# Softmax division moved behind the attention products, and weight splits moved to GpSimd, in a hybrid encoder layer

## The reference, cut to what matters

```python
def _attention(q, k, v):                       # per sequence of 512 tokens, 8 query heads, 2 key/value heads, width 64
    s = jnp.einsum('bqkgd,bskd->bkgqs', qblk, k) * scale
    p = jax.nn.softmax(s, axis=-1)             # exp(s - max) / sum(exp(s - max)) over the 512 keys
    return jnp.einsum('bkgqs,bskd->bqkgd', p, v)
...
attn_out = _attention(q, k, v)
lru_out = h_lru * gelu(gate)                   # gated recurrence, 512 channels
mixed = concatenate([attn_out, lru_out])       # 1024 channels
x = x + einsum('bse,ed->bsd', mixed, w_out)    # output projection
... # then RMSNorm, a router that lets each of 16 experts choose 64 tokens, and three 1024x1024 products per expert
```

## Time and profile before

| | |
|---|---|
| time, median of 3 runs (lowest to highest) | 1011.89 us (1011.8 to 1012.08) |
| time of the profiled execution | 1012.73 us |
| its span from the first to the last instruction | 1010.7 us |
| PE busy | 981.9 us, 97% of the span |
| DVE, ACT, POOL busy | 830.2, 732.6, 173.2 us |
| granted PE clock over the span | 0.992 |

### The profile page before, as it was taken

The page is one execution under the profiler, slowest core; times in us unless marked ns, Lnnn a source line. Parts: engine busy times, 40 slices in busy tenths (PEclk is TensorE's granted clock), DMA queues, the critical chain, the costliest instruction groups (busy, mean ns, idle before and its releaser), DMA issues.

```text
span 1010.7 us, 15239 instructions
## 1 busy us (share of the span) xinstructions
PE 981.9 (97%) x5076; PEld 826.8 (82%) x5076; DVE 830.2 (82%) x1063; ACT 732.6 (72%) x982; POOL 173.2 (17%) x195
## 2 busy tenths in 40 slices
PE   8999999999999999969999999999999999999997
PEld 8997998877878788857888888888888888888885
DVE  6659898989885543667989998999999899989995
ACT  7447897487994334447878887888888788878873
POOL 1000000043793321250100110110011001101001
PEclk9999999999999999979999999999999999999999
DMA  7110111001102635379999999999999999999972
GB/s 269 49 43 21 37 38 43 1 1 64 63 2 66 213 121 177 118 267 398 409 391 392 390 412 392 392 393 409 392 392 405 397 392 391 410 392 392 390 273 62
DMA packets 75315, 248.98 MB, mean 246 GB/s; under 512 B 9421, under 2 KB 16649, under 8 KB 75273
## 3 DMA queue, kind: packets, MB, share of 16 engines
q1 hardware_dynamic: 70472, 231.12, 59.0%
q0 software_dynamic: 4784, 17.30, 6.5%
q10 hardware_dynamic: 16, 0.00, 0.0%
HBM read 231.63 MB, written 16.78 MB: 246 GB/s over the span
## 4 chain that ended last, share of the span: by engine, by line
PE 87%; DVE 5%; ACT 3%; DMA 2%; issue 2%; POOL 1%; POOLq 0%; ACTq 0%; DVEq 0%
PE bank L1097 25%; PE bank L1099 25%; PE bank L1098 25%; PE bank L1103 6%; DMA raw_gate<-in_exp_w_gate_dram 2%; PE bank L1263 1%; PE bank L1262 1%; PE bank L1295 1%; POOL prob L667 1%; DVE e_lo L1905 1%; PE bank L1147 1%; PE bank L1402 1%; POOL wo_lo L659 0%; DVE row_stat L1713 0%; ACT e_hi L1025 0%
## 5 line engine op out<-in xcount | busy, mean ns | idle before, releaser
L1097 PE MATMUL bank<-e_hi,xsT_hi 128*128 128x512 f32 x508 | 199.7, 393 | 1.3 <-DVE e_lo L1905 1.3
L1099 PE MATMUL bank<-e_hi,xsT_lo 128*128 128x512 f32 x508 | 197.8, 389 | 0.0
L1098 PE MATMUL bank<-e_lo,xsT_hi 128*128 128x512 f32 x508 | 197.8, 389 | 0.0
L1025 ACT ACTIVATE e_hi<-raw_gate 128x1024 fp32r<-128x1024 f32 x128 | 134.8, 1061 | 35.0 <-PE bank L1099 29.3
L1905 DVE TENSOR_TENSOR e_lo<-raw_gate,e_hi 128x1024 fp32r<-128x1024 f32 x126 | 149.5, 1221 | 6.1 <-ACT e_hi L1025 2.3
L1905 DVE TENSOR_TENSOR e_lo<-raw_down,e_hi 128x1024 fp32r<-128x1024 f32 x128 | 149.5, 1220 | 4.4 <-ACT e_hi L1025 1.4
L1905 DVE TENSOR_TENSOR e_lo<-raw_up,e_hi 128x1024 fp32r<-128x1024 f32 x128 | 148.4, 1220 | 4.5 <-ACT e_hi L1025 3.2
L1025 ACT ACTIVATE e_hi<-raw_down 128x1024 fp32r<-128x1024 f32 x128 | 128.4, 1060 | 11.8 <-PE bank L1099 11.8
L1025 ACT ACTIVATE e_hi<-raw_up 128x1024 fp32r<-128x1024 f32 x128 | 126.8, 1057 | 2.7 <-PE bank L1099 1.2
L1097 PEld LDWEIGHTS bank<-e_hi,xsT_hi 128*128 128x128 f32 x508 | 95.4, 188 | 22.1 <-DVE e_lo L1905 3.0
L1099 PEld LDWEIGHTS bank<-e_hi,xsT_lo 128*128 128x128 f32 x508 | 95.4, 188 | 19.9
(11 more groups left out here) (305 smaller groups left out, 2022.2 us busy)
## 6 DMA issues: line engine op xcount, KB each, us to landing
raw_gate<-in_exp_w_gate_dram SPq DMA_DIRECT2D x64, 1024.0 KB, 18.2
raw_up<-in_exp_w_up_dram SPq DMA_DIRECT2D x64, 1024.0 KB, 18.8
raw_down<-in_exp_w_down_dram SPq DMA_DIRECT2D x64, 1024.0 KB, 18.5
w_raw<-in_w_in_dram SPq DMA_DIRECT2D x6, 1024.0 KB, 5.4
wo_raw<-in_w_out_dram SPq DMA_DIRECT2D x8, 512.0 KB, 4.3
y_dram<-x SPq DMA_DIRECT2D x8, 512.0 KB, 5.2
h_rows<-h SPq DMA_DIRECT2D x8, 512.0 KB, 2.7
x_nat<-in_x_prompt_dram SPq DMA_DIRECT2D x4, 512.0 KB, 6.0
```

Source lines behind the costliest of these rows:

```text
L1025: act.activation(e_hi[:, (8 * m + j) % SPLIT, :], raw[:, j // 2, j % 2, :], ACT.Copy).then_inc(row_hi, inc)
L1097: pe.matmul(out, l_hi, r_hi, start=first, stop=False)
L1098: pe.matmul(out, l_hi, r_lo, start=False, stop=False)
L1099: return pe.matmul(out, l_lo, r_hi, start=False, stop=last)
```

## The change

The probabilities stay unnormalised: POOL no longer touches `prob`, and the transposes wait for the exponentials (`exp_done`). The division moves behind the products, once per pair. DVE takes the reciprocals of 8 units in one instruction; POOL spreads them over the head width (`spread_recip`); PE turns them, four transposes per pair (`spread_shares`, at the end of slot 8p + 15 for pair p); ACT copies them to `shares` (slot 8p + 16, in place of `mixA_hi`); and DVE multiplies the pair's bank by them into `high_half` (slot 8p + 17). POOL then makes `mixA_hi` and `mixA_lo` from `high_half`. `V_LAG` becomes 9. The high parts of the first 12 halves of `wo` and of the 8 pieces of `lru_out` move from ACT to POOL. Some semaphores of single engines are merged, which adds and removes no work.

```diff
-    T_LAG, V_LAG = 6, 8
+    T_LAG, V_LAG = 6, 9
+    SHARES_AT = {8 * pair + 6 + V_LAG: pair for pair in range(HEADS // 2)}
+    def shares_bank(pair):
+        return 7 if pair < PAIRS_ONE_BANK else out_bank(pair - 1)
+    def ended_pair(u):
+        v = u - V_LAG - 1
+        return v // (2 * BPS) if 0 <= v < UNITS and v % (2 * BPS) == 2 * BPS - 1 else None
...
 # POOL (link: wait for its own last instruction)
+        def spread_recip(pair):
+            pool.wait_ge(recip_done, pair + 1)
+            if pair:
+                pool.wait_ge(high_done, pair)
+            pool.tensor_copy(spread, shares_of.unsqueeze(3).to_broadcast([P, BPS, 2, HD])).then_inc(spread_done, 1)
+        def finish_pair(pair):
+            pool.wait_ge(high_done, pair + 1)
+            link(pool.tensor_copy(mixA_hi[mix_of(pair)], high_half[:, :]))
+            pool.tensor_tensor(mixA_lo[mix_of(pair)], high_half[:, :], mixA_hi[mix_of(pair)].bitcast(F32), ALU.subtract).then_inc(mixA_lo_done, 1)
...
-                pool.wait_ge(wo_hi_done, n + 1)
+                pool.wait_ge(wo_loaded[k], 16)
+                link(pool.tensor_copy(wo_hi[k][:, cols], wo_raw[k][:, cols]))
                 pool.tensor_tensor(wo_lo[k][:, cols], wo_raw[k][:, cols], wo_hi[k][:, cols].bitcast(F32), ALU.subtract).then_inc(wo_lo_pool, 1)
...
-                pool.wait_ge(mixL_hi_done, n - 2 * WO_EARLY + 1)
+                link(pool.tensor_copy(mixL_hi[:, i, cols], lru_out[:, i, cols]))
...
-                pool.wait_ge(recip_done, u + 1)
-                pool.tensor_scalar(prob[:, u % PROB_SLOTS, :], prob[:, u % PROB_SLOTS, :], row_stat[:, 2, u:u + 1], 1.0,
-                                   ALU.mult, ALU.mult).then_inc(prob_done, 1)
+            elif kind == "slot" and ended_pair(n - 1) is not None:
+                finish_pair(ended_pair(n - 1))
+            elif kind == "slot" and n + 4 in SHARES_AT:
+                spread_recip(SHARES_AT[n + 4])
...
 # ACT
-                    act.activation(mixA_hi[...], bank[:, out_bank(pair), :], ACT.Copy).then_inc(mixA_hi_done, 1)
+                    act.wait_ge(shares_turned, pair + 1)
+                    act.activation(shares[:, :], bank[:, shares_bank(pair), :], ACT.Copy).then_inc(shares_copied, 1)
...
 # PE
+                shared = sum(slot < slot_of_turn(n) + 1 for slot in SHARES_AT)    # in turn_heads
+                if shared:
+                    pe.wait_ge(shares_copied, shared)
...
-                pe.wait_ge(mixA_lo_done, pair if pair < PAIRS_ONE_BANK else pair - 1)
+                pe.wait_ge(high_done, pair if pair < PAIRS_ONE_BANK else pair - 1)
+                if pair >= PAIRS_ONE_BANK:
+                    pe.wait_ge(shares_copied, pair)
...
+        def spread_shares(pair):
+            pe.wait_ge(spread_done, pair + 1)
+            if shares_bank(pair) == 7:
+                before = [n for n in range(EARLY, USES * NB) if slot_of_turn(n) < 8 * pair + 6 + V_LAG]
+                pe.wait_ge(*turn_out(before[-1]))
+                pe.wait_ge(*turn_out(before[-2]))
+            else:
+                pe.wait_ge(high_done, pair)
+            transposes(shares_bank(pair), [spread[:, qb, :, :].rearrange("p h d -> p (h d)") for qb in range(BPS)], shares_turned)
...
-                    pe.wait_ge(prob_done, BPS * (head + 1))
+                    pe.wait_ge(exp_done, BPS * (head + 1))
...
 # DVE
-                    dve.tensor_tensor(mixA_lo[where], bank[:, out_bank(pair), :], mixA_hi[where].bitcast(F32), ALU.subtract).then_inc(mixA_lo_done, 1)
-                if 0 <= u - 1 < UNITS:
-                    dve.reciprocal(row_stat[:, 2, u - 1:u], row_stat[:, 1, u - 1:u]).then_inc(recip_done, 1)
+                    dve.wait_ge(pv_done, 2 * BPS * (pair + 1))
+                    dve.wait_ge(shares_copied, pair + 1)
+                    dve.tensor_tensor(high_half[:, :], bank[:, out_bank(pair), :], shares[:, :], ALU.mult).then_inc(high_done, 1)
+                if 0 < u - 1 <= UNITS and (u - 1) % (2 * BPS) == 0:
+                    dve.reciprocal(row_stat[:, 2, units], row_stat[:, 1, units]).then_inc(recip_done, 1)
```

More of the change, by code:

```diff
@@ L163, in layer_program @@
     assert VW * BPS * 4 == 5 * K
+    high_half = at("high_half", R1 + 95 * K, [P, S], F32)
+    shares = at("shares", R6 + 36 * K + 768, [P, S], F32)
+    spread = shares[:, :].rearrange("p (q h d) -> p q h d", q=BPS, h=2)
+    assert 3 * SEQS * HQ * BPS * 4 <= 768 and R6 + 38 * K + 768 <= nc.sbuf_usable_end - base
     QUIET = R1 + 48 * K
@@ L472, in out_bank, with mix_of @@
         return 6 if pair < PAIRS_ONE_BANK or pair % 2 == 0 else 7
+    def shares_bank(pair):
[3 more added lines that the diff above has]
+        return v // (2 * BPS) if 0 <= v < UNITS and v % (2 * BPS) == 2 * BPS - 1 else None
+    def mix_of(pair):
+        return slice(None), pair % (HQ // 2), slice(pair // (HQ // 2) * S, (pair // (HQ // 2) + 1) * S)
     def late_pair(v):
@@ L654, in _, with link @@
                 pool.memset(v[:, :, :].bitcast(F32).rearrange("p b (g d) -> p b g d", d=HD)[:, :, 0::2, :], 0.0).then_inc(v_zeroed, 1)
+        own = [0]
+        def link(ins):
+            own[0] += 1
+            ins.then_inc(pool_step, 1)
+            pool.wait_ge(pool_step, own[0])
+        def spread_recip(pair):
+            pool.wait_ge(recip_done, pair + 1)
+            if pair:
+                pool.wait_ge(high_done, pair)
+            shares_of = row_stat[:, 2, 2 * BPS * pair:2 * BPS * (pair + 1)].rearrange("p (h q) -> p q h", h=2)
+            pool.tensor_copy(spread, shares_of.unsqueeze(3).to_broadcast([P, BPS, 2, HD])).then_inc(spread_done, 1)
[3 more added lines that the diff above has]
+            pool.tensor_tensor(mixA_lo[mix_of(pair)], high_half[:, :], mixA_hi[mix_of(pair)].bitcast(F32), ALU.subtract).then_inc(mixA_lo_done, 1)
         for kind, n in attn:
@@ L923, in _ @@
                 act.activation(small[:, 122:123], eps, ACT.Exp)
-            elif kind == "split_hi":
-                if n < 2 * WO_EARLY:
-                    split_wo_hi(n // 2, n % 2)
-                else:
-                    i, cols = (n - 2 * WO_EARLY) // 2, slice(n % 2 * S, (n % 2 + 1) * S)
-                    act.wait_ge(scores_done, BPS * HQ)
-                    act.wait_ge(gated, SEQS * CT)
-                    act.activation(mixL_hi[:, i, cols], lru_out[:, i, cols], ACT.Copy).then_inc(mixL_hi_done, 1)
-            elif kind == "slot":
-                u, t, v = n, n - T_LAG, n - V_LAG - 1
-                if v >= 0 and v % (2 * BPS) == 2 * BPS - 1:
-                    pair = v // (2 * BPS)
-                    head = 2 * pair
-                    act.wait_ge(pv_done, v + 1)
-                    act.activation(mixA_hi[:, head % HQ // 2, head // HQ * S:(head // HQ + 1) * S], bank[:, out_bank(pair), :],
-                                   ACT.Copy).then_inc(mixA_hi_done, 1)
+            elif kind == "slot":
+                u, t, pair = n, n - T_LAG, SHARES_AT.get(n - 1)
+                if pair is not None:
+                    act.wait_ge(shares_turned, pair + 1)
+                    if pair:
+                        act.wait_ge(high_done, pair)
+                    act.activation(shares[:, :], bank[:, shares_bank(pair), :], ACT.Copy).then_inc(shares_copied, 1)
                 if t == 0:
@@ L1709, in _ @@
             elif kind == "slot":
-                u, t, v = n, n - T_LAG, n - V_LAG - 1
+                u, t, pair = n, n - T_LAG, ended_pair(n)
                 if u < UNITS:
@@ L1713, in _ @@
                     dve.tensor_reduce(row_stat[:, 0, u:u + 1], bank[:, u % SCORE_BANKS, :], AX_X, ALU.max, negate=True).then_inc(max_done, 1)
-                if v >= 0 and v % (2 * BPS) == 2 * BPS - 1:
-                    pair = v // (2 * BPS)
-                    head = 2 * pair
-                    dve.wait_ge(mixA_hi_done, pair + 1)
-                    where = (slice(None), head % HQ // 2, slice(head // HQ * S, (head // HQ + 1) * S))
-                    dve.tensor_tensor(mixA_lo[where], bank[:, out_bank(pair), :], mixA_hi[where].bitcast(F32), ALU.subtract).then_inc(mixA_lo_done, 1)
-                if 0 <= u - 1 < UNITS:
-                    dve.wait_ge(exp_done, u)
-                    dve.reciprocal(row_stat[:, 2, u - 1:u], row_stat[:, 1, u - 1:u]).then_inc(recip_done, 1)
+                if pair is not None:
+                    dve.wait_ge(pv_done, 2 * BPS * (pair + 1))
+                    dve.wait_ge(shares_copied, pair + 1)
+                    if pair:
+                        dve.wait_ge(mixA_lo_done, pair)
+                    dve.tensor_tensor(high_half[:, :], bank[:, out_bank(pair), :], shares[:, :], ALU.mult).then_inc(high_done, 1)
+                if 0 < u - 1 <= UNITS and (u - 1) % (2 * BPS) == 0:
+                    units = slice(u - 1 - 2 * BPS, u - 1)
+                    dve.wait_ge(exp_done, u - 1)
+                    dve.reciprocal(row_stat[:, 2, units], row_stat[:, 1, units]).then_inc(recip_done, 1)
                 if 0 <= t < UNITS:
```

36 lines of the change are left out of this document (20 added, 16 removed).

## The result

The changed kernel takes 1016.04 us in the median of 7 runs (1015.43 to 1017.75), the kernel before 1012.08 us in as many runs beside it (1011.46 to 1012.71). The ratio is 1.0043, 95% interval 1.0031 to 1.0054: slower by some 4 us. The forecast was 1015.2 us, 3.3 us slower.

What follows compares the result with a forecast made beforehand. PE, busy 97% of the span, was taken as the bound. Terms 2.5 + 2.6 - 2.6 + 0 + 0.8 gave +3.3 us on the 1011.89 median: 1015.2 us, range 1012.5 to 1018.2.

Steps and rivals of the forecast that it cites:

- End of pair 0: PE's start of pair 1 waits for high_half behind other work in DVE's queue; same work done 2.37 us later.
- End of pair 1: Same queue delay, 1.68 us, plus 0.8 carried over from the first; PE 2.5 us later in all, not added to 2.37.
- that sign: PE waiting 0.5 us or more for DVE's high_half at the first product of pair 2.
- Middle: Six more groups of four transposes cost PE 2.6 us; vanished waits for POOL's prob and for ACT give 2.6 back.
- POOL: POOL's splits and spreads are ready 1.2 us before PE asks for pair 6's turned shares; 0 us, thin cover.
- rival D: POOL becomes the bound, its copy taking 0.9 us; PE waits 4.3 us at pairs 5 and 6; 1019.5 us, chance 0.13.
- End: Nothing covers the wait between the last product and piece 6: 2.53 us lost instead of 1.80, +0.7, plus 0.1.
- contention: At the end, POOL's copy and subtraction beside DVE's wo_lo add 0.1 us, bounds 0 and 0.5.
- Rival B: No measurable change: same picture with half the loss at the pair ends; 1013.4 us, chance 0.27.
- rival C: Faster: DVE's queue runs ahead and high_half finds DVE idle; -2.4 us, 1009.5 us, chance 0.08.
- The shares transposes' first wait: At pair 0's turned shares PE waits over 1 us for bank 7, and so for ACT's copy.
- The slots of 1.60 us: Sign: from unit 32 to 63 PE's slots take 1.60 us, with eight of 2.03, and no wait for POOL.

Runs made afterwards that it cites:

- e1: Changed kernel with DVE's high_half one slot earlier in its order, behind probT_lo and ahead of v_lo: 1014.40 us, ratio 1.0019.
- e9: Kernel before the change with one number edited, products 9 slots behind the scores instead of 8: 1017.09 us, ratio 1.0046.
- e2: Changed kernel with one of the four shares transposes of each pair, three quarters of the turned shares left out: 1013.85 us, ratio 1.0016.
- e8: Changed kernel once more with no edit: 1016.19 us, ratio 1.0037.
- e11: Changed kernel with POOL's last cast and subtraction held until DVE's four wo_lo are done: 1016.05 us, ratio 1.0031.
- e6: Changed kernel with DVE's four wo_lo of pieces 6 and 7 ahead of the last high_half: 1014.21 us, ratio 1.0017.
- e12: Changed kernel with products 8 slots behind, shares turned two slots earlier, and four wo_lo ahead of the last high_half: 1009.63 us, ratio 0.9975.
- e7: Changed kernel with 8 slots, shares turned two slots earlier, high_half one slot earlier, and four wo_lo ahead of the last high_half: 1010.97 us, ratio 0.9987.

## Why the prediction was right, point by point

**End of pair 0: forecast 2.37 us later.** Before, PE had this work done 30.73 us after its first scores (233.78 - 203.05), now 32.92 (237.03 - 204.11): 2.19 later. Pair 1 starts 31.44 us after the first scores, forecast 31.60. The working of the step, queue place by queue place, held within 0.2 us. e1 shows the cause. e9 shows that it is the ninth slot, which moves the end of a pair behind `v_lo`, and nothing of the shares: the step has this right, in that it counts the turned shares as free there, and e2 confirms it (product 8 at +3.04 with one turn as with four).

**End of pair 1: forecast 2.5.** 252.82 - 204.11 = 48.71 after, 249.47 - 203.05 = 46.42 before: 2.29. The wait there is short, 0.26 us where 0.5 or more was named as a sign: that sign failed. DVE's maximum of unit 25 comes 0.64 us later (249.99 - 204.11 against 248.29 - 203.05), where 0.8 was taken with no more than a guess behind it.

**Middle: +2.6 and -2.6, forecast 0.** At equal work it is -0.1 between products 16 and 63 (2.2 and 2.1 late), with six groups of turned shares between them. e2 shows the positive term, 0.34 us for three of four transposes of a pair. The waits for POOL are gone, and the negative term is what is left: no run takes it alone.

**POOL: forecast 0.** Three of POOL's groups from 202 to 340 us, by line and shape:

```profile
L713 POOL TENSOR_TENSOR mixL_lo<-lru_out,mixL_hi 128x512 fp32r<-128x512 f32 x8 | 10.3, 1294 | 0.6
L706 POOL CAST wo_hi<-wo_raw 128x512 fp32r<-128x512 f32 x12 | 7.4, 613 | 0.0
...
L694 POOL COPY shares<-row_stat 128x512 f32<-128x512 f32 x8 | 4.9, 614 | 14.7 <-DVE row_stat L1779 14.7
```

The copy of 512 takes 0.61 us, where 0.69 was taken, so the cover was thicker than thought, and rival D fell. The Trainium skill (GPSIMD Engine Reference, Elementwise — side-by-side cycle accounting), by which a copy of 512 takes 769 ns at best, is not borne out: 613 ns. (By that figure the forecast would have been 1015.2 + 0.9 = 1016.1, not the 1016.0 written there.)

**End: forecast +0.7 and +0.1; this is the term that was mis-sized.** The first part held: 2.56 us lost between the last matmul and piece 6 where 1.80 were, +0.76. The second, contention, was taken at 0.1 with 0.5 as its upper bound. It measured 1.1 without a fallen clock (block 1 at +3.98, less the 2.1 at product 63 and the 0.76): the third and fourth `wo_lo` come so late that piece 7 waits as well, 0.85 us in e8. In the execution whose clock fell, another 0.8 came on top, which the prediction did not have at all. The Trainium skill (SBUF — State Buffer, Who interferes with whom) says that a DVE instruction with two SBUF inputs contends with a GpSimd instruction that reads SBUF; the trace agrees, 4.20 us against 2.48 in e11, and I gave it too little weight.

**Sum.** 2.3 - 0.2 + 1.9 = 4.0 us up to block 1 against 3.3 forecast (the -0.2 is from the end of pair 1 to product 63); the medians say 4.0 and 3.6 (1016.04 - 1012.08, 1016.19 - 1012.59). That the first of them is met so well is in part luck, as the executions differ behind block 1 too. Rival B, half the loss at the pair ends, and rival C, `high_half` at an idle DVE, both needed DVE to come to the maximum of unit 17 by a microsecond or more earlier; it came 0.43 us earlier (234.22 - 204.11 = 30.11 against 233.59 - 203.05 = 30.54), where 0.3 was taken. The shares transposes' first wait, forecast at over 1 us, was 0.99. The slots of 1.60 us are in the trace (scores of units 30 and 31 at 258.50 and 260.09), but not eight longer ones from unit 32 to 63: the shares of pair 2 are turned at 261.69, just ahead of unit 32, and those of pairs 3 to 6 behind it, the last at 314.54. Eight is the number for the whole stage; the sum took six and had this right.

## What to carry to other kernels

A software pipeline's lag is a place in every engine's queue. Adding a slot by itself made the first product of pair 1 as late as the whole change did (3.09 us, e9), because it put the instruction that frees a bank behind three others, and took from the last product the work that covered it; so, before adding a slot, look what then stands ahead of the instruction that frees something and behind the last one.

An added group on the busiest engine costs its whole length where that engine has no gap and nothing where it waits: count it stretch by stretch. At the end of a stage, put the splits that the next stage needs ahead of the last result (e6 and e12). And an edit that pays at one lag need not pay at another: `high_half` one place earlier gave 1.6 us with 9 slots (e1), and with 8 the version without it has the better median (e12 against e7).

## What the runs showed of the hardware

- DVE's two-input subtraction of 128x512 from SBUF takes 0.62 us back to back with POOL idle (2.48 for four), and 1.05 on average beside POOL's cast and subtraction (4.20 for four); POOL's instructions stretch as well, 0.62 to 1.01 and 1.27 to 1.60 us.
- The granted clock fell for 3.4 us behind a stretch in which PE was busy 1.60 us of 4.00, in one profiled execution of the changed kernel and not in another whose stretch was the same (e8). Of six executions with the same wait of 2.40 us it fell in two. The fall cost 0.8 us there; in e7 a fall in the ramp and a wait 0.85 us longer came with 2.2 us together. So the cost of a wait of some 2 us has a part that differs from one execution to the next.
